# In the decode's last batch, VectorE makes the low value parts from the fifth piece on

## What is computed

```python
def fox_sample(q, k_new, v_new, logf_new, k_past, v_past, logf_past):
    ...
    s = jnp.einsum('bqhd,bkhd->bhqk', q, k_all, preferred_element_type=F32) * FOX_SCALE
    s = s + cq[..., :, None] - c[:, :, None, :]
    s = jnp.where(kpos[None, :] <= qpos[:, None], s, -jnp.inf)
    p = jax.nn.softmax(s, axis=-1).astype(v_all.dtype)
    return jnp.einsum('bhqk,bkhd->bqhd', p, v_all)
```

## Time and profile before

| | |
|---|---|
| median of 3 runs | 2382.87 us (2380.59 to 2383.26) |
| profiled execution | 2386.91 us, span 2384.8 us |
| mean granted clock of TensorE | 0.968 |
| TensorE busy | 2229.5 us, 93% |
| VectorE busy | 997.5 us, 42% |
| ScalarE busy | 914.7 us, 38% |
| GpSimd busy | 626.6 us, 26% |
| `dec_v_lo` by GpSimd | 92 instructions, 239.1 us, mean 2618 ns |

### The profile page before, as it was taken

The page is one execution under the profiler, slowest core; times in us unless marked ns, Lnnn a source line. Parts: engine busy times, 40 slices in busy tenths (PEclk is TensorE's granted clock), DMA queues, the critical chain, the costliest instruction groups (busy, mean ns, idle before and its releaser), DMA issues. The chain is left out here.

```text
span 2384.8 us, 30909 instructions
## 1 busy us (share of the span) xinstructions
PE 2229.5 (93%) x11248; PEld 1810.3 (76%) x11248; DVE 997.5 (42%) x1511; ACT 914.7 (38%) x1460; POOL 626.6 (26%) x380
## 2 busy tenths in 40 slices
PE   7999999899999787999999799699999999998999
PEld 7999999767777675767777478477777878886787
DVE  4343444453844756777787710410022222223211
ACT  5333333223443433777777520422223443334200
POOL 1311122220220000556666741121112221113300
PEclk9999999999999888999999899699999999999999
DMA  5222232202201113999999553422221223223531
GB/s 155 43 55 50 54 76 65 58 9 63 63 1 45 31 71 111 350 331 331 323 328 317 182 170 97 161 95 91 75 96 56 81 100 107 81 74 103 173 106 53
DMA packets 257403, 287.95 MB, mean 121 GB/s; under 512 B 69562, under 2 KB 168764, under 8 KB 257148
## 3 DMA queue, kind: packets, MB, share of 16 engines
q1 hardware_dynamic: 240538, 252.78, 33.7%
q10 hardware_dynamic: 16738, 33.53, 3.8%
HBM read 246.03 MB, written 41.26 MB: 120 GB/s over the span
## 5 line engine op out<-in xcount | busy, mean ns | idle before, releaser
L226 PE MATMUL bank<-whi,x_hi 128*128 128x512 f32 (+1 forms) x1536 | 592.7, 386 | 21.3 <-POOL wlo L206 16.1
L228 PE MATMUL bank<-wlo,x_hi 128*128 128x512 f32 (+1 forms) x1536 | 579.7, 377 | 0.0
L230 PE MATMUL bank<-whi,x_lo 128*128 128x512 f32 (+1 forms) x1536 | 578.6, 377 | 0.0
L226 PEld LDWEIGHTS bank<-whi,x_hi 128*128 128x128 f32 x1536 | 292.5, 190 | 83.5 <-POOL wlo L206 20.7
L259 ACT ACTIVATE projected<-bank 128x512 f32<-128x512 f32 (+1 forms) x160 | 92.2, 576 | 610.5 <-PE bank L230 581.4
L230 PEld LDWEIGHTS bank<-whi,x_lo 128*128 128x128 f32 x1536 | 292.9, 191 | 41.8
L228 PEld LDWEIGHTS bank<-wlo,x_hi 128*128 128x128 f32 x1536 | 293.2, 191 | 39.2 <-issue 0.7
L2317 POOL TENSOR_TENSOR dec_v_lo<-dec_v,dec_v_hi 128x1024 fp32r<-128x1024 f32 x92 | 239.1, 2618 | 196.0 <-ACT dec_v_hi L2674 195.9
L206 POOL TENSOR_TENSOR wlo<-wraw,whi 128x512 fp32r<-128x512 f32 (+1 forms) x192 | 231.5, 1238 | 44.5 <-ACT whi L199 44.5
L2489 DVE TENSOR_TENSOR dec_kt_lo<-bank,dec_kt_hi 128x512 fp32r<-128x512 f32 x256 | 168.5, 683 | 82.1 <-ACT dec_kt_hi L2664 81.0
L2664 ACT ACTIVATE dec_kt_hi<-bank 128x512 fp32r<-128x512 f32 x256 | 144.5, 593 | 105.9 <-PE bank L2345 105.0
(11 more groups left out here) (372 smaller groups left out, 3449.8 us busy)
## 6 DMA issues: line engine op xcount, KB each, us to landing
dec_k<-cache_k SPq DMA_DIRECT2D x256, 256.0 KB, 3.9
dec_v<-cache_v SPq DMA_DIRECT2D x256, 256.0 KB, 4.2
wraw<-w_in_even SPq DMA_DIRECT2D x32, 512.0 KB, 6.8
wraw<-w_in_odd SPq DMA_DIRECT2D x16, 1024.0 KB, 8.6
gv<-projected ACTq DMA_DIRECT2D x4, 2304.0 KB, 8.0
gm_v<-gv SPq DMA_DIRECT2D x8, 1152.0 KB, 6.0
m<-gm_mt ACTq DMA_DIRECT2D x8, 1056.0 KB, 4.1
wraw<-w_in_odd SPq DMA_DIRECT2D x4, 2048.0 KB, 8.7
```

What stands on the lines that cost most here:

```text
L226: pe.matmul(bank[:, 0:width], e.xhi[:, k, c:c + P], e.whi[:, k, 0:width], start=(k == 0), stop=False)
L228: pe.matmul(bank[:, 0:width], e.xhi[:, k, c:c + P], e.wlo[:, k, 0:width], start=False, stop=False)
L230: mm = pe.matmul(bank[:, 0:width], e.xlo[:, k, c:c + P], e.whi[:, k, 0:width], start=False, stop=(k == KD - 1))
```

## The change

In the last batch (r = DB - 1) VectorE makes the low parts of pieces 1, 3 and 4 to 15; GpSimd makes those of pieces 0 and 2 and goes on to the output stage's slices. The waits of TensorE and SyncE for low parts follow `on_vector`, so they now ask for VectorE's count. Nothing else is changed, and the results are the same.

```diff
 def on_vector(r, p):
 
-    return p % 4 == 3 if r < DB - 1 else p % 2 == 1
+    return p % 4 == 3 if r < DB - 1 else p % 2 == 1 or p >= 4
```

## The result

| | before | after |
|---|---|---|
| median | 2382.85 us (22 runs, 2379.33 to 2386.62) | 2379.61 us (22 runs, 2375.68 to 2384.45) |
| ratio after / before | | 0.9987, interval [0.9981, 0.9993] |
| span of the profiled execution | 2384.8 us | 2380.1 us |
| GpSimd busy | 626.6 us | 604.9 us |
| VectorE busy | 997.5 us | 990.9 us |

By the ratio the kernel is 3.1 us faster, with an interval of 1.7 to 4.5 us (0.0013 of 2382.85, and the ends of the ratio); the medians lie 3.24 us apart. The forecast was 1.9 us, and "within 0.2%" held. One run of an experiment further down (hold_loads, 5961.72 us) counts as slow and is left out of its ratio.

The account below looks back on a forecast made before the run. TensorE, busy 93%, bounds the kernel; the change is worth what it moves slice 5's arrival. -3.0 (heads' chain) - 0.4 (earlier loads) + 1.5 (clock fall) = -1.9 us, giving 2381.0 us; range 2377.0 to 2384.0.

Parts of the forecast that it names:

- within 0.2%: Whole kernel: the measured change would be under about 4.8 us either way; chance 0.79.
- The pieces and the alternation: Last batch: VectorE and GpSimd take turns, 3.33 us a pair; with GpSimd silent VectorE needs 1.2 us a piece.
- the slower rival: Last batch: a piece costs VectorE 3.33 us even with GpSimd silent; kernel takes 2398.5 us; chance 0.05.
- The opening of the output stage: Second low part of m ends at 1357.56 instead of 1362.26, 4.7 us earlier, before any gain from earlier loads.
- the lead d: SyncE reaches the output stage's first load up to 1.7 us earlier; 0.4 taken as reaching the data, DMA queue nearly full.
- the lock: Heads' addition (L2576), two SBUF inputs, waits out GpSimd's slice 2: about 1.9 us long, chain moves 3.0 instead of 4.7.
- My own sign of being wrong: Listed as refuting the forecast: m's first load landing as much earlier as it is issued.
- The gap and the clock: Ahead of slice 5 TensorE idles about 3.1 us, then runs at half clock, losing 1.5 us.
- Before nothing was lost: In the kernel before, the clock stayed at 1.00 after the 1.44 us gap at slice 5, so no cost there.
- The bound's 3.4 us: Clock cost behind slice 5's gap: bounds 0 and 1.7 us, the upper being half of 3.4 us.
- clock kept: Rival: the clock does not fall after the gap at slice 5; -3.4 us, 2379.5 us; chance 0.18.
- much of the queue's lead: Rival: the full 1.7 us of SyncE's earlier loads arrives; -3.2 us, 2379.7 us; chance 0.10.

Follow-up runs that it names:

- hold_loads: Changed kernel with one more SyncE wait, so the output stage's first load is issued only after piece 11's high part: 2380.46 us, ratio 0.9985.
- the second execution: Another profiled execution of the changed kernel itself, run beside the others on one chip, nothing edited: 2380.14 us, ratio 0.9986.
- psum_both: Changed kernel, but in the last batch the second reduction's result, the small addition's result and thus the scaling's input lie in PSUM: 2378.84 us, ratio 0.9979.

## Why the prediction was right, and where it was off

**The pieces and the alternation**: as forecast. 1.2 us a piece beside a silent GpSimd; the slower rival, that 3.4 us was VectorE's own, is out.

**The opening of the output stage:** forecast 4.7 us plus the lead d for the second low part of m; measured 5.9 (33.52 to 27.63) and 5.6. The addition: forecast about 1.9 us long by the lock, measured 1.84 and 1.85. The end of the addition then moved by 4.25 and 3.93 us, 3.0 plus 1.25 and 0.93 for d; slice 5 by 4.7 and 5.0. What it gained beyond the store (0.4 and 1.0 us) lies in its load, 5.0 us from issue to high part before, 4.6 and 4.0 after; the prediction had no term for it, and its cause is open. Nor is it shown that the hold costs the kernel the 1.7 us between 3.0 and 4.7: with the hold gone, the store lay 5.5 us earlier than before, but the read-back only 4.3, where with the hold it lay 4.2 and 3.9.

**The term that was mis-sized is d.** I read the DMA engines' share of 0.93 at 307 GB/s as a nearly full queue and gave the lead 0.4 us; it was 1.4 us (21.82 to 20.43), and 1.1 in the second execution. The engines moved up to 385 GB/s at shares that hardly differ; and the trace of before already had 392 GB/s at a share of 1.04, from 943 to 948 us, where the cache is loaded too. I also had the wrong link for it: not SyncE's earlier arrival at m's load counts, but that the values' loads ahead of it start earlier. My own sign of being wrong was there: in the first execution m's load was issued 1.56 us earlier and its high part started 1.39 us earlier. A clock of 1.00 behind the gap, in the second, was another.

**The gap and the clock:** forecast a gap of 3.1 us and 1.5 us for the clock. The gap was 2.14 and 1.58, for two reasons: the quicker load of slice 5, and that TensorE reached slice 5 5.4 and 5.1 us earlier while the second low part of m came 5.9 and 5.6 earlier, its half clock at the opening lasting longer. "Before nothing was lost" holds at slice 5 only; the earlier fall was overlooked. The clock fell at slice 5 in one of the two executions, and cost 1.61 us there; the price was right and its occasion was not, since it rested on a gap of 3.73 us. (The bound's 3.4 us is how long the clock stayed at 0.50 there, 926.3 to 929.7.) As a cost in every run the term was too sure; in the mean of many it is somewhere between the two, which the medians can't resolve.

Together, from the traces: slice 5 moved by 4.7 us and the clock gave 1.6 of it back in one execution (the samples moved by 3.1), and 5.0 with nothing given back in the other. From the mark to the end of the span the two executions are 2.4 and 4.4 us shorter than the one of before, and the median's 3.1 lies between. The forecast of 1.9 lay 1.2 us under it, and the misjudged lead alone is 0.7 to 1.0 of that. That these parts make the median's 3.1 is worked out, not shown: the interval of the ratio is as wide as each of them. The mechanism was right, but the number owes something to a wide range: 2379.6 is where two of the rivals stood (clock kept, 2379.5; much of the queue's lead, 2379.7), and the traces show some of each.

## What to carry to other kernels

When VectorE and GpSimd show equal long durations side by side, compare the ends: if each ends a fixed time behind the other, they take turns, and work may be better placed on the fast one alone: here a pair fell from 3.33 us to 2.33 (4.65 for four). But then ask what small operation will next meet GpSimd's long instruction; here a 32 x 64 addition took 1.6 us longer, freeing it handed the wait to the scaling behind it, and moving the work up handed it to the low part of m. Freeing both moved the store, but hardly the load that waits for it: follow a gain to the last link before you count it. And don't take a DMA share near 1 for a limit: look at the GB/s that the same kind of load reaches elsewhere, with more of them in flight.

## What the runs showed of the hardware

- The granted clock can fall at a gap much shorter than the 3.73 us on which the forecast rested, and need not fall at one nearly as long. At slice 5: gaps of 2.14, 2.15, 2.35 and 2.98 us went with a clock of 0.50 (in the last it fell within the gap) and with 21.4, 21.4, 21.4 and 22.5 us to the samples; gaps of 1.30, 1.44, 1.58 and 2.06 us did not, at 19.8 us each, nor did one of 1.50, at 20.2. At the opening of the output stage the clock fell in all twelve traces: around a gap of 2.3 to 2.5 us with the change or its last four pieces; and in the kernel before behind gaps of 1.1 us between the pieces and one of 1.81, at 1359.8, before the gap of 1.90. So the length of the last gap alone does not tell.
- A `tensor_scalar` on a 32 x 64 fp32 tensor in SBUF waits for GpSimd just as an addition of two such tensors does (1.57 us against 0.24); with its tensor input in PSUM it does not (0.27 us in psum_both, with GpSimd at work).
- A load can land earlier though it is issued later: from its issue to the start of the high part made from it, m's first load took 5.4 us when held (14.57 to 19.97 us behind the mark) and 6.9 us when not (13.53 to 20.43).
